# A decoder layer on one core: the expert route made tile by tile inside the w_co projection, with lists of 1024 places per expert

## What is computed

```python
x = x + cross_attention(...)           # its last step: @ w_co
xt = rms_norm(x, norm_ffn_g)
logits = xt @ w_router + b_router
top_vals, top_idx = lax.top_k(logits, TOP_K)
gates = jax.nn.softmax(top_vals, axis=-1)
# assignments sorted by expert; each block of rows has one expert
hid = x_pad[tok] @ w1[e] + b1[e]
y = clamped_swiglu(hid) @ w2[e] + b2[e]
out = segment_sum(y * gate, row_tok)   # x + out, then a last rms_norm
```

## Time and profile before

| | us |
|---|---|
| median of 3 runs (3435.72 to 3442.59) | 3436.45 |
| the profiled execution | 3427.17 |
| its span | 3425.5 |
| TensorE busy in the span | 2913.8 (85%) |
| VectorE busy | 1148.8 (34%) |
| GpSimd busy | 500.8 (15%) |

### The profile page before, as it was taken

One profiled execution on the slowest core, in us unless ns is written; L12 is line 12 of the kernel. 1 busy time (PEld: TensorE's weight loads), 2 busy tenths in 40 slices (PEclk: granted clock), 3 DMA queues, 4 the chain that ended last, 5 costly groups with the idle time before them and its releaser, 6 DMA issues. The chain is left out here.

```text
span 3425.5 us, 54810 instructions
## 1 busy us (share of the span) xinstructions
PE 2913.8 (85%) x20974; PEld 2739.6 (80%) x20975; DVE 1148.8 (34%) x2439; ACT 669.2 (20%) x1261; POOL 500.8 (15%) x577
## 2 busy tenths in 40 slices
PE   7899888398999397986359999999999999999990
PEld 6876774288888396886359999999999999999990
DVE  2128221744443432232312222223222322232227
ACT  3139213111211312222001111111111111111111
POOL 0000001122213000001141110111111111111103
PEclk9999998699999698998579999999999999999995
DMA  6100210000000112014148877788888888888777
GB/s 223 32 25 1 56 43 7 0 1 0 0 0 0 51 55 69 12 56 151 53 135 298 286 269 270 270 292 294 291 292 293 288 297 286 292 294 276 270 260 260
DMA packets 320781, 543.61 MB, mean 159 GB/s; under 512 B 23584, under 2 KB 102176, under 8 KB 320672
## 3 DMA queue, kind: packets, MB, share of 16 engines
q1 hardware_dynamic: 301344, 499.67, 42.4%
q0 software_dynamic: 19360, 42.87, 4.1%
HBM read 506.01 MB, written 36.47 MB: 158 GB/s over the span
## 5 line engine op out<-in xcount | busy, mean ns | idle before, releaser
L2124 PE MATMUL experts_up<-experts_xs,g_pieces 128*128 128x144 f32 (+1 forms) x8192 | 1034.3, 290 | 114.4 <-DVE experts_xs L2053 77.4
L2124 PEld LDWEIGHTS experts_up<-experts_xs,g_pieces 128*128 128x128 f32 x8192 | 1027.7, 197 | 121.2 <-issue 121.2
L2147 PE MATMUL experts_down<-experts_hs,g_across 128*128 128x144 f32 (+1 forms) x3072 | 389.2, 289 | 0.0
L2147 PEld LDWEIGHTS experts_down<-experts_hs,g_across 128*128 128x128 f32 x3072 | 386.1, 190 | 0.0
L2002 POOL DMA_INDIRECT experts_x<-h_rows,experts_index x198 | 192.3, 971 | 1133.5 <-DVE experts_xs L2053 1078.6
L2083 DVE TENSOR_SCALAR experts_glu<-experts_up,experts_bias 128x176 f32<-128x176 f32 x256 | 102.3, 400 | 710.1 <-PE experts_up L2124 710.1
L2033 ACT ACTIVATE experts_sig<-experts_glu 128x352 f32<-128x352 f32 x128 | 63.7, 497 | 998.4 <-DVE experts_lin L2085 998.4
L2040 ACT ACTIVATE experts_yT<-experts_down,experts_bias 128x176 f32<-128x176 f32 x256 | 104.2, 407 | 381.1 <-PE experts_down L2147 305.8
L989 POOL TENSOR_TENSOR chunk_part<-chunk_corr,rwkv_level_mask 128x1024 f32<-128x1024 f32 x56 | 119.2, 2128 | 351.9 <-DVE chunk_corr L1078 188.5
L2074 DVE COPY experts_bias<-g_bias 128x24 f32 x32 | 5.8, 181 | 391.7 <-ACT experts_yT L2040 391.6
L2136 PE MATMUL experts_down<-experts_hs,g_across 128*128 128x144 f32 (+1 forms) x1024 | 133.3, 289 | 0.0
(11 more groups left out here) (377 smaller groups left out, 4408.1 us busy)
## 6 DMA issues: line engine op xcount, KB each, us to landing
g_pieces<-in_w_dram SPq DMA_DIRECT2D x132, 2048.0 KB, 8.1
g_across<-in_w_dram SPq DMA_DIRECT2D x64, 2048.0 KB, 9.3
y_rows<-experts_y SPq DMA_DIRECT2D x132, 192.0 KB, 3.9
g_across<-in_w_ckv_dram SPq DMA_DIRECT2D x8, 1024.0 KB, 10.2
rkv_raw<-in_w_in_dram SPq DMA_DIRECT2D x13, 512.0 KB, 3.9
diff_qk_raw<-in_w_in_dram SPq DMA_DIRECT2D x9, 512.0 KB, 4.0
cross_q_raw<-in_w_cq_dram SPq DMA_DIRECT2D x9, 512.0 KB, 4.3
m_u<-in_x_dram SPq DMA_DIRECT2D x8, 512.0 KB, 10.1
```

Of the source, the lines that this page charges most:

```text
L2124: ins = pe.matmul(up[:, u % 4, l * N:l * N + w], raw[c][:, k, at:at + 255:2], xs[:, k, 0:w], start=(k == 0), stop=(k == 7), skip_group_che ...
L2147: ins = pe.matmul(down[:, n % 4, 0:w], raw[4 + n // 4][:, k, (n % 4) * P:(n % 4 + 1) * P], hs[:, k, 0:w], start=(k == 0), stop=(k == 7), s ...
```

## The change

first_pieces, turn_biases and route are gone as stages. project_norm_route does their work within the w_co block.

- The step loop of the last column part has two more places: at step s TensorE also makes the logits of tile s - 3 and the ranks of tile s - 4, and VectorE selects tile s - 3 (`select`) and places tile s - 4 (`enlist`). GpSimd scatters a tile's token numbers as soon as its places are there, four indirect DMAs for a tile.
- So that a place is known before the counts of all tiles are, each expert has a list of its own with ROOM = 1024 places; `row_token` has 33024 entries in place of 4480. The gather reads where a window's list starts from a new table R.source. The results stay dense: R.offset and R.row are made at the end, R.row by one more product over the marks of the chosen experts.
- The tables over the windows have one window per partition (operations of 32 elements), are spread on a diagonal and brought to all partitions by one product with ones (`table`).
- `product` has two banks in place of four; the regrouped rows, the gains and ScalarE's scrap output lie in the buffers of the raw weights, so that the gains are loaded after the last weights are split.
- b1 and b2 are loaded behind the first weight piece and turned before the first product. The w1 pieces of the first expert are asked for at the start of the experts' block.

```diff
-def route(nc, I, hT, row_token, R, C):
...
+ROOM = T_ALL
+LISTED = -(-(NE * ROOM + SLOTS) // P) * P
+def project_norm_route(nc, I, across, x, h_rows, row_token, R, C):
...
+        quarters = raw[:, 0].rearrange("p k n -> p (k n)").rearrange("p (j n) -> p j n", n=D)
+        spare = raw[:, 1].rearrange("p k n -> p (k n)").rearrange("p (j n) -> p j n", n=D)
+        junk, gains = spare[:, 0], spare[:, 1]
...
+        product = S.ps("product", [P, 2, 512])
+        flipped = S.ps("flipped", [P, 2, D])
...
+                part(0)
+                sp.dma_start(b1_rows, I["b1"][0]).then_inc(b_in, 16)
+                sp.dma_start(b2_rows, I["b2"][0]).then_inc(b_in, 16)
+                part(1)
+                sp.dma_start(weights[:], I["w_router"][0].rearrange("(k p) n -> p k n", p=P)).then_inc(router_in, 16)
+                sp.dma_start(base[:], row_to_all(I["b_router"][0])).then_inc(base_in, 16)
+                sp.wait_ge(made.sem, made.value("zeros"))
+                sp.dma_start(row_token.rearrange("(p n) a -> p (n a)", p=P), zeros[:]).then_inc(cleared, 16)
+                part(2)
+                part(3)
+                sp.wait_ge(dve_steps.sem, dve_steps.value(f"w{LAST}"))
+                sp.dma_start(gains, row_to_all(I["norm_ffn_g"][0])).then_inc(gain_in, 16)
+                for t in range(TT):
+                    sp.wait_ge(regrouped, t + 1)
+                    sp.dma_start(h_rows[t * P:(t + 1) * P, :], quarters[:, t % 2, :]).then_inc(rows_out[t % 2], 16)
...
+                def select(t):
+                    if t == 0:
+                        dve.wait_ge(base_in, 16)
+                        dve.wait_ge(made.sem, made.end())
+                    dve.wait_ge(pe_steps.sem, pe_steps.value(f"logits{t}"))
+                    dve.tensor_tensor(logits[:, t, :], logit[:, t % 2, :], base[:], ALU.add).then_inc(*dve_steps.step(f"logits{t}"))
+                    follows()
+                    dve.max(best[:, t, :], logits[:, t, :]).then_inc(*dve_steps.step(f"best{t}"))
+                    follows()
+                    dve.max_index(index[:, t, :], best[:, t, :], logits[:, t, :]).then_inc(*dve_steps.step(f"index{t}"))
+                    follows()
+                    dve.tensor_copy(index_f[:, t, :], index[:, t, 0:TOPK]).then_inc(*dve_steps.step(f"float{t}"))
+                    dve.tensor_tensor(gates[:, t, :], best[:, t, 0:TOPK], best[:, t, 0:1].to_broadcast([P, TOPK]),
+                                      ALU.subtract).then_inc(*dve_steps.step(f"lead{t}"))
+                    follows()
+                    dve.tensor_tensor(chosen[:, t], number[:].unsqueeze(1).to_broadcast([P, TOPK, NE]),
+                                      index_f[:, t, :].unsqueeze(2).to_broadcast([P, TOPK, NE]), ALU.is_equal).then_inc(*dve_steps.step(f"chosen{t}"))
+                    follows()
+                    dve.tensor_reduce(member[:, t, :], chosen[:, t].rearrange("p j e -> p e j"), AX, ALU.add).then_inc(*dve_steps.step(f"member{t}"))
+                    follows()
+                    dve.tensor_tensor(before[:, t + 1, :], before[:, t, :], member[:, t, :], ALU.add).then_inc(*dve_steps.step(f"before{t}"))
+                def enlist(t):
+                    dve.wait_ge(pe_steps.sem, pe_steps.value(f"rank{t}"))
+                    dve.tensor_tensor(place[:, t % 2, :], rank[:, t % 2, :], room[:], ALU.add).then_inc(*dve_steps.step(f"place{t}"))
+                    follows()
+                    dve.tensor_tensor(spot[:, t % 2], chosen[:, t], place[:, t % 2, :].unsqueeze(1).to_broadcast([P, TOPK, NE]),
+                                      ALU.mult).then_inc(*dve_steps.step(f"spot{t}"))
+                    follows()
+                    dve.tensor_reduce(dest[:, t, :], spot[:, t % 2], AX, ALU.add).then_inc(*dve_steps.step(f"dest{t}"))
+                    follows()
+                    dve.tensor_copy(spot_at[:, t, :], dest[:, t, :]).then_inc(*dve_steps.step(f"at{t}"))
...
+                weights_low(1)
+                dve.wait_ge(pe_steps.sem, pe_steps.value("biases"))
+                dve.tensor_copy(R.bias[:, 0:16, :], flipped[:, 0, 0:512].rearrange("p (n e) -> p n e", e=NE)).then_inc(*dve_steps.step("bias_up"))
+                dve.tensor_copy(R.bias[:, 16:24, :], flipped[:, 0, 512:768].rearrange("p (n e) -> p n e", e=NE)).then_inc(*dve_steps.step("bias_down"))
...
+                for s in steps_of:
+                    if s < TT:
+                        add(LAST, s)
+                    if 0 <= s - 1 < TT:
+                        normalise(s - 1)
+                    if 0 <= s - 3 < TT:
+                        select(s - 3)
+                    if 0 <= s - 4 < TT:
+                        enlist(s - 4)
...
+                dve.tensor_scalar(begun[:], first[:, 1:NE + 1], window[:, 0:1], None, ALU.is_le).then_inc(*dve_steps.step("begun"))
+                follows()
+                dve.tensor_reduce(column[:, 0:1], begun[:], AX, ALU.add).then_inc(*dve_steps.step("owner"))
+                dve.tensor_tensor(moved[:, 0, :], begun[:], shift[:, 0, :], ALU.mult).then_inc(*dve_steps.step("moved"))
...
+                for n in range(3):
+                    dve.tensor_scalar(diagonal[:, n, :], C.ident[:, 0:TABLE], column[:, n:n + 1], None, ALU.mult).then_inc(*dve_steps.step(f"diagonal{n}"))
...
+                dve.tensor_tensor(chosen[:].rearrange("p t j e -> p (t j) e"), chosen[:].rearrange("p t j e -> p (t j) e"),
+                                  shift[:, 2, :].unsqueeze(1).to_broadcast([P, TT * TOPK, NE]), ALU.mult).then_inc(*dve_steps.step("spots"))
...
+                dve.wait_ge(pe_steps.sem, pe_steps.value("table"))
+                dve.tensor_copy(R.owner[:], table[:, 0, :]).then_inc(*dve_steps.step("owner_int"))
+                dve.tensor_scalar(R.offset[:], table[:, 1, :], float(WINDOW), None, ALU.add).then_inc(*dve_steps.step("offset_int"))
+                dve.tensor_copy(R.source[:], table[:, 2, :]).then_inc(*dve_steps.step("source_int"))
...
+                    if n >= 2:
+                        pe.wait_ge(dve_steps.sem, dve_steps.value(cell((n - 2) // TT, (n - 2) % TT)))
+                    to = product[:, n % 2, 0:COLS]
...
+                pe.wait_ge(b_in, 32)
...
+                for s in steps_of:
+                    if s < TT:
+                        products(LAST, s)
+                    if 0 <= s - 2 < TT:
+                        t = s - 2
+                        pe.wait_ge(dve_steps.sem, dve_steps.value(f"rows{t}"))
...
+                            ins = pe.transpose(flipped[:, t % 2, k * P:(k + 1) * P], rows[:, t % 2, k * P:(k + 1) * P], C.ident[:])
+                        ins.then_inc(*pe_steps.step(f"turn{t}"))
+                    if 0 <= s - 3 < TT:
+                        t = s - 3
+                        pe.wait_ge(act_steps.sem, act_steps.value(f"out{t}"))
+                        if t == 0:
+                            pe.wait_ge(router_in, 16)
+                        if t >= 1:
+                            pe.wait_ge(dve_steps.sem, dve_steps.value(f"logits{t - 1}"))
+                        for k in range(8):
+                            ins = pe.matmul(logit[:, t % 2, :], across[:, k, t * P:(t + 1) * P], weights[:, k, :], start=(k == 0), stop=(k == 7))
+                        ins.then_inc(*pe_steps.step(f"logits{t}"))
+                    if 0 <= s - 4 < TT:
+                        t = s - 4
+                        if t == 0:
+                            pe.wait_ge(made.sem, made.end())
+                        pe.wait_ge(dve_steps.sem, dve_steps.value(f"before{t}"))
+                        if t >= 1:
+                            pe.wait_ge(dve_steps.sem, dve_steps.value(f"place{t - 1}"))
+                        pe.matmul(rank[:, t % 2, :], earlier[:], member[:, t, :], start=True, stop=False)
+                        pe.matmul(rank[:, t % 2, :], ones[:], before[:, t, :], start=False, stop=True).then_inc(*pe_steps.step(f"rank{t}"))
+                pe.wait_ge(dve_steps.sem, dve_steps.value(f"place{TT - 1}"))
...
+                for s in range(1, TT + 4):
+                    if 0 <= s - 1 < TT:
+                        t = s - 1
+                        pool.wait_ge(dve_steps.sem, dve_steps.value(f"rows{t}"))
+                        if t >= 2:
+                            pool.wait_ge(rows_out[t % 2], 16 * (t // 2))
+                        for q in range(4):
+                            ins = pool.tensor_copy(quarters[:, t % 2, q * 256:(q + 1) * 256].rearrange("p (c i) -> p c i", i=32),
+                                                   rows[:, t % 2, :].rearrange("p (c b i) -> p b c i", b=4, i=32)[:, q])
+                        ins.then_inc(regrouped, 1)
+                    if 0 <= s - 4 < TT:
+                        t = s - 4
+                        pool.wait_ge(dve_steps.sem, dve_steps.value(f"at{t}"))
+                        for j in range(TOPK):
```

(18 more changed lines are left out.)

497 lines of the change are left out of this document (248 added, 249 removed).

## The result

The changed kernel takes 3379.41 us (median of 4 runs, 3378.16 to 3381.26) against 3436.52 us of the kernel before beside it: a ratio of 0.983, with an interval of 0.9813 to 0.9848. It is faster by 57 us where I had forecast 86.5, and lies outside my range of 3339 to 3367. The profiled execution took 3381.26 us (span 3379.7) against 3427.17, so in the two profiles 45.9 us were saved and 40.6 of the forecast are missing. By the medians 29 are missing; the profiled execution of the kernel before was 9.3 us under its median, that of the changed kernel 1.9 over. On another chip the same changed kernel was measured against the kernel before at 0.9804 (0.9788 to 0.9821), 3362.05 against 3428.65 us; that comparison is the base for the experiments. That 3362 lies within my range is no success of the forecast: the kernel before was faster there too, and the step that failed fails there as well.

What follows compares the result with a forecast made beforehand. A 154 us TensorE hole, ended by one chain making the route, was taken as the bound; moving the first expert product from 1753.86 to 1667.3 us saves 86.5, giving 3349.9 us from 3436.45, range 3339 to 3367.

Steps and rivals of the forecast that it cites:

- Delay ahead of it: Before the last column part of w_co: with two product banks TensorE waits 3.7 us, once, for the first add.
- T: Start of the last column part of the w_co projection, forecast at 1568.4 us; later steps are dated from it.
- request to first product: From the first list's request to the first expert product: 16.7 us as before plus 4.8 for queues loaded with weights.
- the allowance for contention: GpSimd's scatters in the last part: 3 us added for VectorE's work beside them, bounds 0 and 5.4.
- rival 2: Last part: each scatter waits for a whole VectorE operation, 18.7 us in place of 3; 16 less saved, 3366; 6%.
- rival 5: Last part: nothing overlapped, positions come only after the projection; 25 us less saved, 3375; 2%.
- rival 3: Last part: TensorE falls to 1.2 GHz, a step takes 11.8 us; 36 less saved, 3386; 4%.
- rival 4: Expert windows: padding rows from one address stretch the gathers beyond their slack; slower than before, 3444 and up; 1%.
- rival 1: Experts' start: first list and rows starve behind 12.6 MB of weights, 47 us for 21.5; 26 less saved, 3376; 8%.
- Landing 2.8 as before: After the last scatter in the last column part: the scatters land in 2.8 us, as in the earlier trace.
- the block change at 0.5 us: Turn from the projection's block to the experts' block, ahead of GpSimd's memset: 0.5 us, an estimate.
- the queues: Experts' start: the weights' load delays the first list by 2.5 us and rows about as much, 4.8 in all.

Runs made afterwards that it cites:

- e5: The changed kernel again, unedited, on another chip; gap from last scatter to the experts' memset 19.9 us; no separate time or ratio is given for this run.
- e6: Changed kernel without the GpSimd drain, plus two one-element memset marks around the wait for the scatters; gap 15.6 us, no time or ratio given.
- e7: Changed kernel with the drain kept, plus the same two one-element memset marks on GpSimd; gap 18.3 us, no time or ratio given.

## Why the prediction was wrong

The direction and the mechanism were right, and most terms held; the landing, taken over from the kernel before, was off by 11 to 17 us, and two smaller ones by 3 to 4 each. By the steps of the prediction, in the two profiles:

| step | forecast | measured | late |
|---|---|---|---|
| what comes ahead of the stage | 0 | 3.8 | 3.8 |
| *Delay ahead of it* | 3.7 | 7.0 | 3.3 |
| last part to the last scatter's end | T + 73.2 | T + 72.1 | -1.1 |
| landing and block change | 3.3 | 22.3 | 19.0 |
| memset to the list's request | 0.9 | 2.2 | 1.3 |
| request to first product | 21.5 | 25.1 | 3.6 |
| 31 windows | 0 | 10.6 | 10.6 |

The sum is 40.5 of the 40.6 us.

*Right: the last part.* VectorE's adds in the changed kernel, in the steps that have all the work:

```profile
1593.41 0.42 DVE L1785 TENSOR_TENSOR g_x<-g_x,w_co_product 128x256 f32<-128x256 f32 x1 [0.75 <-PE w_co_product L1948]
1599.40 0.42 DVE L1785 TENSOR_TENSOR g_x<-g_x,w_co_product 128x256 f32<-128x256 f32 x1 [0.23 <-PE w_co_product L1948]
1605.56 0.42 DVE L1785 TENSOR_TENSOR g_x<-g_x,w_co_product 128x256 f32<-128x256 f32 x1 [0.41 <-PE w_co_product L1948]
```

They are 6.0 and 6.2 us apart, forecast 6.23. The first list positions were there 23.7 us after the part's start, forecast 24.0, and GpSimd's scatters and regroupings took 48.1 us, forecast 49.2 with 3 us for VectorE beside them. So the step of TensorE, the allowance for contention and the claim that GpSimd sets the end all held. Rivals 2 and 5 did not come (most scatters took 0.96 us as before, the longest 1.50); nor did rival 3, since the clock fell only in the tail (0.96 from 1576 to 1625, 0.50 behind it, 0.81 on the mean of the stretch); nor rival 4, since the windows took 48.5 us in e5. The list landed in 6.46 us beside the weights, so the rows did not starve either (rival 1).

*Wrong: "Landing 2.8 as before".* This is the step that failed. I took the 2.8 us from the earlier trace rows, where the same 32 instructions with the same bytes at the same pace had written a dense list. The change altered nothing in them but the addresses, and I priced the longer list at nothing. It cost 15 us at the end in the marked kernels, some 19 in the first profile, and 1.9 with 4160 bytes between the lists. It does not show in GpSimd's rows, since the scatters' issue is no slower; only the wait behind them pays for it.

*Wrong: the block change at 0.5 us.* The drain is part of it and took 2.9 us behind these scatters. The 0.5 us was an estimate without a row. The request of the list is late as well: it stands 1.65 us behind the memset where I had 0.4, since the register load ahead of the request, which the earlier trace rows had within the 2.81 us that I called landing, now comes behind the memset.

*Wrong by size: the delay ahead.* TensorE's wait for the first add was 2.88 us, where I had 3.7. Of the other 4.2 us, 3.7 are two things that the sum lacked. TensorE did the 24 bias transposes, whose loads had landed only at 1496.20, ahead of its first product: that stood 15.4 us behind the copy of across, against 13.2 before. I had named 1 to 3 us for this and taken 0. And the wait cost more than its length. Here are stretches of TensorE before it, behind it, and from where the clock was back:

```profile
1505.00:1507.00 2.00, 2.00 (x19) 2.00 (x19) 2.00 (x3) 0.00 (x0) 0.00 (x0) 1.00 0.00 0
1511.50:1514.50 3.00, 3.00 (x16) 3.00 (x16) 0.00 (x0) 0.00 (x0) 0.00 (x0) 0.50 0.56 190
1515.00:1518.00 3.00, 3.00 (x27) 3.00 (x26) 0.54 (x2) 0.00 (x0) 0.00 (x0) 1.00 0.00 0
```

The first eight products behind the pause of 2.88 us still took 0.12 us each. Then the granted clock was 0.50, that is 1.2 GHz, from 1511.4 to 1514.8: 16 products at 0.21 us each instead of 0.12, 1.5 us more.

*Wrong by size: the queues.* From the request to the first list's use it took 8.8 us (1672.04 to 1680.85) against 4.2 in the earlier trace rows, and from there to the product 16.3 against 12.5: 4.6 and 3.8, together 8.4 where I had put 2.5 and about as much, 4.8 as the sum had it. Both halves were too low. Even my bound of 5.0 for the list was only just enough. Ordering the pieces takes back 4.4 of the 8.4; what is left is 2.5 us for the list and 1.4 for the rows, beside the one or two pieces that still go first.

*Not of the change.* The 3.8 us ahead of the stage are within the 8.4 us by which executions of this code differ, and the windows' 10.6 us are gone on another chip. They may be why the changed kernel reached 0.9804 there and 0.983 here; the intervals of the two ratios overlap, and whether the kernel before had the halt on the first chip too is not known. Without these two the forecast missed by 26 us in the profile, most of it the landing.

## What to carry to other kernels

When a change moves where small writes go, the time from issue to landing has to be priced anew, even if instruction, size and number stay: look at the distances between the addresses that one scatter writes, and try another one if they are 4096 bytes (here 64 bytes more did it; 1024 and 4160 are the only others that were tried). Read the median time from issue to landing of every DMA that someone waits for at a stage's end, in short stretches, and the time of the packets on its queue, since a backlog does not show on the engine that issues. And if a gap's releaser is only the engine's own sequencer, a mark of one element before and behind each wait tells in one run what guesses about drains and barriers do not.

## What the runs showed of the hardware

- 32 scatters of 128 numbers of 4 bytes, one every 1.26 us or slower, into 32 regions that begin 4096 bytes apart: the landing time grew from 3.9 to 15.5 us (e6). With regions 4160 or 1024 bytes apart the wait behind the last was 1.9 and 1.1 us. The Trainium skill, "DMA: Bandwidth & Descriptors", section "Latency and other measured facts", tells of a loss at power-of-two row pitches in copies of large tiles, for pitches of 2 MiB and more, where 192 bytes of padding did not help and 4 KiB did. Here the pitch is 4 KiB, the writes are of 4 bytes, and 64 bytes of padding were enough; for such writes the measurement decides.
- In the marked kernel without the drain (e6) GpSimd is done with the last scatter at 1645.09. The last packets in the trace come before 1646.0, none from there to 1660.5, and the wait for the landing ends only then. That the trace shows no more packets does not mean that the writes have landed.
- The row stores that ran beside these scatters were slowed too, 4.3 to 4.4 us from issue to landing where it is 2.6 to 2.8 with the other distances.
- A GpSimd drain at a block's end took 2.9 us behind 32 indirect DMAs that had all landed (e7); without it the turn took 0.1 us (e6). It is no fixed price: behind four scatters the whole gap, landing included, was 2.63 us.
- The same program took some 0.3 us more for nearly every window in one profile than in another, 11 us in all; in ten of the 32 windows it is one halt of TensorE of 0.2 us that shows.
